# A planned network kernel on one Trainium2 core: where norms, first weights and evictions stand at the borders of layers

## What is computed

```python
# first block, per layer                       (2 tiles of tokens)
x = x + 0.5 * swiglu(rms_norm(x, g1), w_gate_up, w_down)      # stage f10, f11
x = x + mixers(rms_norm(x, gm) @ w_in) @ w_out                # three sequence mixers
x = x + 0.5 * swiglu(rms_norm(x, g2), w_gate_up, w_down)      # stage f20, f21
x = rms_norm(x, final)                                        # stage rows1
# second block, per layer l                    (4 tiles: x and ctx)
m = silu(c) @ ada_w[l] + ada_b[l]                             # 9 modulation vectors ("ada")
h = rms_norm(t) * (1 + m[3j + 1]) + m[3j]
t = t + 0.5 * m[3j + 2] * swiglu(h, w_gate, w_up, w_down)     # half00, half02, half10, half12
# between them: a Fourier mixer (layer 0: four), a retention mixer (layer 1: ret, retout)
```

## Time and profile before

| | us |
|---|---|
| Median of 3 runs | 3540.86 (3536.08 to 3541.58) |
| Profiled execution | 3534.76 |
| Its span, first to last instruction | 3533.0 |
| TensorE matmul busy | 3284.5 (93%) |
| TensorE weight load busy | 2842.0 (80%) |
| VectorE busy | 2119.1 (60%) |
| ScalarE busy | 1281.6 (36%) |
| Mean granted TensorE clock | 0.968 of full |

### The profile page before, as it was taken

One profiled execution on the slowest core, in us unless ns is written; L12 is line 12 of the kernel. 1 busy time (PEld: TensorE's weight loads), 2 busy tenths in 40 slices (PEclk: granted clock), 3 DMA queues, 4 the chain that ended last, 5 costly groups with the idle time before them and its releaser, 6 DMA issues.

```text
span 3533.0 us, 46024 instructions
## 1 busy us (share of the span) xinstructions
PE 3284.5 (93%) x19058; PEld 2842.0 (80%) x19058; DVE 2119.1 (60%) x2595; ACT 1281.6 (36%) x1521; POOL 123.3 (3%) x126
## 2 busy tenths in 40 slices
PE   7998888999999897999799999999989999899899
PEld 7987877898988786898687877787878788787797
DVE  6858647776866756677774744774343333544554
ACT  4444144444435124543321222322233222443543
POOL 0001200000000220000000000000000000000000
PEclk9999988999999998999899999999999999999999
DMA  6542021565553011456343431343222222232452
GB/s 253 217 157 77 26 86 67 203 238 203 204 212 104 26 60 70 179 221 238 107 172 110 177 113 36 109 171 113 89 80 94 101 84 90 104 105 98 165 186 97
DMA packets 83539, 463.21 MB, mean 131 GB/s; under 512 B 7537, under 2 KB 11249, under 8 KB 43266
## 3 DMA queue, kind: packets, MB, share of 16 engines
q1 hardware_dynamic: 77664, 451.45, 34.6%
q10 hardware_dynamic: 5666, 8.82, 0.8%
HBM read 459.19 MB, written 1.05 MB: 130 GB/s over the span
## 4 chain that ended last, share of the span: by engine, by line
PE 63%; DVE 26%; ACT 8%; issue 2%; POOL 1%; ACTq 0%; DMA 0%; DVEq 0%; POOLq 0%
PE ps L100 62%; DVE lo L307 8%; DVE acc L455 5%; ACT hi L301 3%; PE ps L542 1%; DVE acc L452 0%; DVE m1xc L1679 0%; DVE m0xc L1679 0%; DVE m1restMs L1935 0%; DVE xt L686 0%; POOL st L617 0%; DVEq L86 0%; DVE f21rot L857 0%; DVE f11rot L857 0%; DVE f20rot L857 0%
## 5 line engine op out<-in xcount | busy, mean ns | idle before, releaser
L307 DVE TENSOR_TENSOR lo<-raw,hi 128x2048 fp32r<-128x2048 f32 (+1 forms) x357 | 811.6, 2273 | 668.9 <-ACT hi L301 649.0
L301 ACT ACTIVATE hi<-raw 128x2048 fp32r<-128x2048 f32 (+1 forms) x357 | 676.0, 1894 | 593.7 <-PE ps L100 557.5
L455 DVE SCALAR_TENSOR_TENSOR acc<-raw,sil,acc 128x512 f32<-128x512 f32 x504 | 379.0, 752 | 20.4
L100 PE MATMUL ps<-half02hs,hi 128*128 128x512 f32 x672 | 210.7, 395 | 4.4 <-DVE half02fin L684 4.4
L100 PE MATMUL ps<-half00hs,hi 128*128 128x512 f32 x672 | 210.5, 395 | 4.3 <-DVE half00fin L684 4.3
L100 PE MATMUL ps<-half10hs,hi 128*128 128x512 f32 x672 | 209.6, 393 | 4.4 <-DVE half10fin L684 4.4
L100 PEld LDWEIGHTS ps<-half10hs,hi 128*128 128x128 f32 x672 | 126.5, 189 | 32.0 <-issue 4.8
L100 PEld LDWEIGHTS ps<-half02hs,hi 128*128 128x128 f32 x672 | 126.5, 189 | 31.7 <-issue 4.8
L100 PEld LDWEIGHTS ps<-half00hs,hi 128*128 128x128 f32 x672 | 125.9, 189 | 31.2 <-issue 4.7
L100 PE MATMUL ps<-half02hs,lo 128*128 128x512 f32 x352 | 138.3, 393 | 0.0
L100 PE MATMUL ps<-half10hs,lo 128*128 128x512 f32 x352 | 138.1, 392 | 0.0
(11 more groups left out here) (909 smaller groups left out, 7952.9 us busy)
## 6 DMA issues: line engine op xcount, KB each, us to landing
raw<-in_ffn_w_gate_up SPq DMA_DIRECT2D x88, 1024.0 KB, 9.2
raw<-in_ffn_gu SPq DMA_DIRECT2D x88, 1024.0 KB, 4.9
raw<-in_ffn_w_down SPq DMA_DIRECT2D x85, 1024.0 KB, 5.2
raw<-in_ada_w SPq DMA_DIRECT2D x72, 1024.0 KB, 5.0
raw<-in_w_in_t SPq DMA_DIRECT2D x28, 1024.0 KB, 5.0
raw<-in_ret_w_in SPq DMA_DIRECT2D x24, 1024.0 KB, 4.8
raw<-in_w_out SPq DMA_DIRECT2D x16, 1024.0 KB, 5.0
raw<-in_w_in_n SPq DMA_DIRECT2D x12, 1024.0 KB, 4.9
```

What stands on the lines that cost most here:

```text
L100: return p().matmul(o, l, r, start=start, stop=stop, skip_group_check=True)
L301: a().activation(self.high(w), self.raw[self.place(r)][:, 0:width], ACT.Copy).then_inc(*a.mark(self.wac, w))
L307: v().tensor_tensor(self.low(w), self.raw[self.place(r)][:, 0:width], self.high(w).bitcast(F32), ALU.subtract).then_inc(*v.mark(self.wdv, w))
L455: v().scalar_tensor_tensor(out=acc[:, n, :], in0=w[:, k, :], scalar=s, in1=acc[:, n, :], op0=ALU.mult, op1=ALU.add).then_inc(*v.mark(self. ...
```

## The change

Five edits:

1. `plan`: a spare first tile is split where the tile two before the last has been used (one entry of the list sooner than the tail), and doesn't move the running position `first` of the tiles after it.
2. `Ffn`, four tiles of tokens: the last down tile of the first part gets four phases, one for each tile of tokens, and its evictions come one by one. `hold` keeps the split of the first tile of the second part until the phase of the second tile of tokens. `back` swaps the banks of the first two tiles of tokens there, and the second part's first product waits for the first tile's eviction, its second for the second's.
3. `join` with four tiles: the norm of tile t comes after the sums and eviction of tile t + 1. So it is at four to half02, half02 to half10 and half10 to ret.
4. `join` at f21 to half00: sums 0, rows1 0, sums 1, norm of tile 0, rows1 1, norm of tile 1.
5. `ffn` for f21 alone: an ada phase after three of every four gate-and-up tiles. That is 17 in the loop in place of 15, so `fill_to(18)` adds none.

```diff
@@ plan
             if n == 0 and s.spare is not None:
                 self.hi.append(s.spare)
-                h, before, ahead = len(self.hi) - 1, None, 1
+                self.hislot.append((len(self.hi) - 1, None))
+                self.early[next(i for i, n in enumerate(used) if n + 3 > w)].append(w)
+                continue
             else:
...
                 last[h] = w
+                if n in s.hold:
+                    first = max(first, ends[s.key, s.hold[n]])
@@ Ffn.__init__
+            if k < len(parts) - 1:
+                self.hold[n], ph = ph, ph + nt - 1
@@ Ffn.back
-        return self.K.ps[(other, other + 2, own + 2 * ((last + 1) % 2), own + 2 * (last % 2))[t] + h]
+        return self.K.ps[(other if t < 2 else own) + 2 * ((last + 1 + t) % 2) + h]
@@ Ffn.tensor
                 elif nt == 4 and k:
-                    p.wait_ge(*self.dv["out", k - 1, 1, 1])
+                    p.wait_ge(*self.dv["out", k - 1, j, 1])
...
-                if len(group) > 1:
+                ends = group == self.groups[k][-1]
+                if ends:
                     order = [(a, t) for t in range(nt) for a in parts]
...
-                    if len(group) > 1 and (i, chunk) == parts[-1] and t < nt - 1:
+                    if ends and (i, chunk) == parts[-1] and t < nt - 1:
                         yield
@@ Ffn.vector
-                        if len(g) > 1 and t < self.nt - 1:
+                        if t < self.nt - 1:
                             yield
@@ network
-    def ffn(s, gates=()):
+    def ffn(s, gates=(), soon=False):
...
-                elif j % 3 < 2:
+                elif j % (4 if soon else 3) < (3 if soon else 2):
                     fill()
...
                 if len(g) == 1:
-                    run(s)
+                    for _ in range(s.nt if g == s.groups[k][-1] else 1):
+                        run(s)
...
     def join(s, *norms):
+        norm = norms[-1]
         for t in range(s.tail):
             run(s)
-            for norm in norms:
+            if len(norms) > 1:
+                if t:
+                    run(norm)
+                run(norms[0])
+            elif s.tail < 4 or t:
                 run(norm)
-        run(norms[-1])
+        if s.tail == 4 or len(norms) > 1:
+            run(norm)
+        run(norm)
...
-        ffn(s)
+        ffn(s, soon=(l, which) == (1, 2))
```

More of the change, by code:

```diff
@@ L342 @@
 class Stage:
-    phases, his, places, since, tail, spare, his_first, near = 1, 0, 0, (), 1, None, 0, 5
+    phases, his, places, since, tail, spare, his_first, near, hold = 1, 0, 0, (), 1, None, 0, 5, {}
     def __init__(self, K, kind, who, after=()):
@@ L724, in __init__ @@
         ph, j, n = 0, 0, 0
-        self.groups = []
+        self.groups, self.hold = [], {}
         for k, count in enumerate(parts):
@@ L839, in scalar @@
             for g in self.groups[k]:
-                for _ in range(self.nt if len(g) > 1 else 1):
+                for _ in range(self.nt if g == self.groups[k][-1] else 1):
                     yield
```

## The result

| | before | after |
|---|---|---|
| Median | 3539.39 us (3535.27 to 3543.38, 6 runs) | 3523.70 us (3520.75 to 3529.32, 6 runs) |
| Profiled execution, its span | 3534.76, 3533.0 | 3523.58, 3521.8 |
| Mean granted TensorE clock | 0.968 | 0.968 |

The ratio is 0.9959, 95% interval 0.9948 to 0.997: faster, by 0.4%, which is 15.7 us where 23.7 were forecast. The mean clocks of the two profiled executions are equal, though the change was to win clock at three places. That is the thread to follow.

What follows compares the result with a forecast made beforehand. With the chain 63% TensorE, gains come only where TensorE stands still: -16.0 + 3.3 - 10.0 + 2.6 - 1.95 - 1.65 = -23.7 us, median 3540.9 to 3517, range 3507 to 3532.

Steps and rivals of the forecast that it cites:

- switches, idle: Switch of parts in half00, half02, half10: TensorE restarts 3.64 us sooner each, 10.9 in all, less 0.6 at half10.
- switches, clock: Behind the three switches: the lower TensorE clock after each wait is won back whole, 5.7 us.
- border f21 to half00: Ada phases move into the loop and the last down tile isn't held: TensorE waits 9.35 for 19.4, -10.0 us.
- four to half02: TensorE's sums pace evictions, so a norm behind the next eviction only lengthens the end: +2.6 us.
- half02 to half10, half10 to ret: At these borders the earlier weight split gives all the gain, the order nothing: -1.95 and -1.65 us.
- f21's loop, with the down tiles: In f21's loop, paced by VectorE with its chain over ScalarE, two more ada phases cost 2 x 1.67, +3.3 us.
- missing 0.6 at half10: At half10's switch no short ada matmuls cover VectorE's later finish, so TensorE pays 0.6 us.
- The upper bound of the step, +6.3: f21's loop: two phases of 3.1 us cost in full if ScalarE's lead is won back nowhere.
- Rival (e): f21's loop is paced by something else: phases cost 6.3, border gains only 7; -17.7, 3523 us; chance 8%.
- Rival (a): At the switches the clock isn't won back, falling at any stop of TensorE: -18.0, 3523 us; chance 14%.
- M: Experiments' rival, whole trace: stretches at the lower clock come somewhere in any case, at a later stop if not the switch.

Runs made afterwards that it cites:

- e5_switch: The kernel before with edit 2 alone (a phase for each tile of tokens at the switch of parts): 3524.91 us, ratio 0.996.
- e12: The changed kernel itself run once more, nothing altered: 3526.66 us, ratio 0.997.
- e6_spare: The kernel before with edit 1 alone (first weights of the half stages split a tile sooner): 3532.96 us, ratio 0.9982.
- e7: e4 with the old order of norms also at half02 to half10, half10 to ret, sooner split kept: 3521.26 us, ratio 0.995.
- e4: The changed kernel with the old order at four to half02 alone, each norm straight behind its eviction: 3522.69 us, ratio 0.9952.
- e2_gap: The changed kernel with the same 17 ada phases laid four on, one off, a tile without one before each reduction: 3514.06 us, ratio 0.9935.
- e3_border: The changed kernel with edit 5 undone, two ada phases back from f21's loop at the border f21 to half00: 3518.87 us, ratio 0.9944.
- e1_down: The changed kernel with f21's loop back at two phases of three tiles, two phases put beside its first five down tiles: 3520.04 us, ratio 0.9949.
- e8: e2_gap with the old order of norms at four to half02: 3515.94 us, ratio 0.9932.
- e11: e2_gap with the old order of norms at every border: 3513.55 us, ratio 0.9933.
- e9: e8 without ada phases beside the last gate-and-up tile of a half stage's second part: 3516.03 us, ratio 0.9934.

## Why the prediction was right, and where its size was off

**Step by step.** Forecast, and what the traces of the change and of its parts show:

| step | forecast | measured | from |
|---|---|---|---|
| switches, idle | -10.3 | -11.2 + 0.45 = -10.7 | waits 4.3, 4.4, 4.4 to 0.57, 0.67, 0.67; at half10's second product 0.45 |
| switches, clock | -5.7 | -5.8 | e5_switch, table |
| border f21 to half00 | -10.0 | -9.7 | waits 19.4 to 9.7 |
| four to half02 | +2.6 | +2.5 | 3.7 to 6.2 |
| half02 to half10, half10 to ret | -1.95, -1.65 | -1.7, -1.7 | 9.9 to 8.2, 9.7 to 8.0 |
| f21's loop, with the down tiles | +3.3 | +7.9 | 202.9 to 210.8 (the loop alone 137.8 to 147.9) |

The first six runs were on the lucky side: their median is 15.7 under before, and e12's set of six is 9.1 under the before beside it. The measured steps add up to -19.2, and the means of all runs say -13.1. Of the 6 us between, one is the last step itself, which is +9.0 as the mean of the four profiles that have its pattern; the rest lies outside the steps (below). All steps but one hold to half a us; the median of 3523.7 where the forecast had 3517 is the work of the one that doesn't and of the clock outside the steps. The cause of each was then tested by a run of its own: the switch by e5, the sooner split (all of the gain at half10 and ret, none from the order) by e6 and e7, the order's cost at four by e4. At the switch the forecast's missing 0.6 at half10 came out as 0.45.

**The step that failed** is the sentence "its own work is close behind VectorE's; it has no more in the new loop, and what VectorE takes longer comes out as wait", with "The pattern three on, one off has no step longer than 6.98, so I take 3.3". The pace was read rightly: VectorE's steps are 6.98 in the new loop too (1488.77 to 1495.75), and e2_gap, which has the same phases and no long stop, takes 3.5 more than before to the end of the down tiles' sums. What was left out is where in TensorE's list the reductions stand. Put right behind their sums they hold TensorE, and behind the longest stop VectorE waits in its turn (a step of 9.06, from 1575.02 to 1584.08). It gives somewhat more idle time in fewer and longer stops, and the clock fell behind these. Of what the changed kernel loses, up to 6.0 are idle (3.2 to 9.2) and some 3 clock: 5.0 behind two reductions, less the 1.8 (26 x 0.07) that before lost at the loop's start:

```profile
1474.00:1500.00 26.00, 25.90 (x204) 25.69 (x202) 21.35 (x24) 15.05 (x18) 0.00 (x0) 0.93 0.41 155
```

The upper bound of the step, +6.3, was for another mechanism and didn't reach it. Rival (e) named the loop and gave 3523, which is near the time that was measured; its mechanism was wrong in one half, since the border gained 9.7 and not 7. Rival (a), no clock won, gave 3523 too, and over the whole kernel none was won (121.3 to 121.0 in the table); but its reason was that the switches keep their low, and there the clock is 1.00.

The whole stretch can be read from the profiles to a tenth of a us, from the loop's first matmul over the down tiles' last sums to the first transpose of half00:

| kernel | loop | to the end of the sums | wait | together |
|---|---|---|---|---|
| before, e5_switch | 137.8 | 202.9 | 19.4 | 222.2 |
| e6_spare | 137.8 | 202.9 | 16.0 | 218.9 |
| e3_border | 137.8 | 202.9 | 15.7 | 218.6 |
| after, e12, e4, e7 | 147.9 to 150.2 | 210.8 to 213.0 | 9.7 | 220.5 to 222.7 |
| e1_down | 137.8 | 207.8 | 9.7 | 217.5 |
| e2_gap, e8 to e11 | 140.6 to 140.7 | 206.3 to 206.4 | 9.7 (e11: 10.0) | 216.0 to 216.4 |

The forecast for this stretch was 6.7 us less. The change as it was made gained 1.7 in its first profile and lost 0.5 in e4's; with e2_gap's pattern it gains 6.2, the forecast nearly to the half us. Of the 11 us between the changed kernel and the five, this stretch holds 4 to 7; the rest lies behind half00's first transpose.

A slip in the sum for half02 to half10 did no harm: 2610.1 and a step of 4.4 make 2614.5 and not 2614.8, so the step was -2.25 by its own terms; 1.7 were measured.

**What the sum over the kernel says.** In the table of clocks the mean fell by 13.1 us, the clock's part by 0.3. That part also holds lows in which TensorE stood still and that cost nothing. One is large: in before, in the wait at f21's border,

```profile
1683.00:1697.00 14.00, 0.00 (x0) 0.00 (x0) 6.29 (x11) 6.83 (x18) 2.19 (x4) 0.50 0.00 0
```

14 x 0.50 = 7.0 us of the 121.3 are free; in the changed kernel the same border has

```profile
1682.00:1694.70 12.70, 3.05 (x14) 2.14 (x12) 5.78 (x10) 5.96 (x16) 2.20 (x4) 0.77 0.25 85
```

12.7 x 0.23 = 2.9. So what the clock costs TensorE at work rose by some 4 us (7.0 - 2.9 - 0.3), and the idle time fell by 17. In the profiles TensorE's idle time (span less busy) is 248.5 us in before, 235.0 in after and 231.9 in e12, 13.5 and 16.6 less. The forecast for all but the clock was -18.0, and for the clock -5.7. The first was nearly right and the second was -5.8 at the switches, as forecast, and about +10 elsewhere: 119.9, the mean of the 20 runs that have the three-of-four pattern, against 109.3 of the five with e2_gap's. (e3_border and e1_down, with the old pattern in the loop, have 111.9 and 113.3.)

**What stays open.** The two stretches in the loop hold 5 of these 10. Others lie at stops that every kernel has. The clock behind the 1.39 stop is 1.00 in before and in e6_spare, which have the old switch, 0.76 in e5, e2 and e12, and 0.58 in after. So a longer time without a low ahead of it goes with a low there, which is a correlation in a dozen profiles and no more. M has this much for it; no run took a stop away without moving another, as e9 shows.

And some lows stand behind no stop at all. In after, at the end of the Fourier stage, TensorE is busy in the profile for 17 us without a pause and then has a clock of 0.69; before, as busy at the same place, has 1.00 (two stretches of after, then one of before):

```profile
2190.00:2207.00 17.00, 17.00 (x63) 10.72 (x61) 4.33 (x7) 1.45 (x4) 0.00 (x0) 1.00 0.20 64
2207.00:2218.00 11.00, 11.00 (x27) 6.52 (x27) 5.72 (x11) 3.69 (x9) 1.10 (x2) 0.69 0.00 1
```

```profile
2190.00:2221.00 31.00, 31.00 (x110) 18.93 (x108) 16.54 (x23) 9.79 (x18) 1.64 (x3) 1.00 0.20 68
```

So the lows are not a matter of stops alone, and what else brings them no run here shows.

The Trainium skill (TensorE: Matmul & The Clock Gate, A second HAM failure mode) tells of a kernel in which TensorE idles briefly between groups of matmuls, often enough that its clock goes down and up, and that loses throughput by it. The lows here behind 1.39 us of wait agree with it in kind; the same wait in before and the seven waits for `lo` in e2_gap's loop, of 0.3 to 1.3 us, both with a clock of 1.00, do not.

## What to carry to other kernels

When work is moved within a loop, follow every instruction that it brings to each engine, and look at what stands directly ahead of it in that engine's list: here a reduction of 1.8 us, put right behind the sums that it reads, made long stops out of idle time that was for the most part there anyway. In this loop the idle time was cheaper in nine short stops than in a few long ones, because TensorE's clock fell behind the two longest (2.3 and 3.9 us) in all four profiles; that this holds elsewhere isn't shown. Sort the waits by the longest as well as by the total. And a norm placed behind the next tile's eviction gives nothing where the eviction waits for TensorE, or where VectorE has no pause to fill: the sooner split (e6_spare) and the earlier eviction (e5_switch) were worth 20 us together, the order less than nothing.

## What the runs showed of the hardware

The same stop (1.39 us for `mods`, with the same matmuls ahead of it and behind) was followed by a granted clock of 1.00, 0.76 or 0.58 over 7 us, depending on the kernel and, for one kernel, on the execution (after and its repetition: 0.58 and 0.76). So the price of a stop can't be read from one profile. Nor does a low need a stop: the clock fell to 0.69 over 11 us behind 17 us in which TensorE had no pause. Executions of one kernel differ by some 9 to 11 us, and kernels whose waits differ by 3 us can't be told apart by five runs. The mean granted clock of each run, averaged over runs, was the better witness: it put 10 us on the clock where the medians only said that something was off.
